# Forgetting attention: the requests' forget sums in a buffer of their own, split later, and the last quarter of output tile 0 moved

## The reference, cut to what matters

```
logf  = log_sigmoid(f_raw + f_bias)
f_cum = cumsum(concat([past_logf, logf], axis=1), axis=1)
s = einsum('bqhd,bkhd->bhqk', q, k) * scale
s = s + f_cum[query] - f_cum[key];  s = where(key <= query, s, -inf)
out = einsum('bhqk,bkhd->bqhd', softmax(s), v)
...
out = concat([c_out, d_out]) @ w_out
```

## Time and profile before

| | |
|---|---|
| median of three runs | 1737.83 us |
| lowest and highest run | 1737.72 and 1738.06 us |
| span of the profiled execution | 1735.7 us |
| mean granted TensorE clock in it | 1.000 |
| TensorE busy (matmul) | 98% of the span, 11360 instructions |
| VectorE, ScalarE, GpSimd busy | 61%, 39%, 21% |

### The profile page before, as it was taken

How to read it: one execution, slowest core, us unless ns; L and a number is a source line. 1 busy time by engine, 2 the same in 40 slices (tenths; PEclk the granted TensorE clock), 3 DMA queues, 4 the chain that set the end, 5 groups by cost and what they waited for, 6 DMA issues and landing times.

```text
span 1735.7 us, 27688 instructions
## 1 busy us (share of the span) xinstructions
PE 1702.0 (98%) x11360; PEld 1543.0 (89%) x11360; DVE 1058.7 (61%) x1717; ACT 683.9 (39%) x1219; POOL 370.5 (21%) x289
## 2 busy tenths in 40 slices
PE   7999998999999999999999999999999999999999
PEld 6566556797999999999989899789899999999999
DVE  3699867637667647465654424744676774655574
ACT  4111243435525525253552124633543453544352
POOL 3012100211104324132213132200110241414240
PEclk9999999999999999999999999999999999999999
DMA  8222330142303131403143221603320313122212
GB/s 263 101 77 103 93 107 28 49 195 98 104 27 138 32 130 46 135 19 128 31 141 74 75 73 64 246 27 114 153 93 25 128 48 115 61 70 86 87 66 91
DMA packets 39674, 162.30 MB, mean 94 GB/s; under 512 B 9384, under 2 KB 10280, under 8 KB 25600
## 3 DMA queue, kind: packets, MB, share of 16 engines
q1 hardware_dynamic: 32240, 124.59, 21.5%
q0 software_dynamic: 7312, 35.98, 5.8%
HBM read 149.87 MB, written 10.42 MB: 92 GB/s over the span
## 4 chain that ended last, share of the span: by engine, by line
PE 92%; DVE 5%; ACT 2%; issue 1%; DMA 0%; POOL 0%; SPq 0%; DVEq 0%; ACTq 0%
PE G L940 68%; PE S L940 11%; PE Q L940 11%; PE Q L1635 1%; ACT work L1731 0%; DVE rstd L2344 0%; DMA ring<-in_w_mk 0%; DVE ev_low L2593 0%; ACT rstd L1731 0%; DVE stats L2623 0%; DVE resid L2875 0%; ACT h_split L1731 0%; PE Q L1347 0%; DVE stats L2992 0%; DVE work L2636 0%
## 5 line engine op out<-in xcount | busy, mean ns | idle before, releaser
L940 PE MATMUL G<-ffn_rows,w_split 128*128 128x320 f32 x2160 | 329.8, 309 | 0.0
L940 PEld LDWEIGHTS G<-ffn_rows,w_split 128*128 128x128 f32 x2160 | 320.1, 188 | 0.0
L1731 ACT ACTIVATE w_split<-ring 128x512 fp32r<-128x512 f32 (+2 forms) x224 | 159.1, 711 | 316.8 <-PE G L940 208.4
L940 PE MATMUL G<-front,ring 128*128 128x128 f32 (+2 forms) x832 | 223.3, 430 | 11.0 <-DMA ring<-in_w_mk 9.3
L940 PEld LDWEIGHTS G<-front,ring 128*128 128x128 f32 x832 | 133.0, 193 | 100.0 <-issue 95.9
L856 POOL TENSOR_TENSOR mkT<-ring 128x512 f32<-128x512 f32 x72 | 98.2, 1369 | 564.6 <-DMA ring<-in_w_up 382.2
L940 PE MATMUL G<-h_split,w_split 128*128 128x320 f32 x1344 | 200.9, 310 | 1.2 <-DVE w_split L2359 0.8
L940 PEld LDWEIGHTS G<-h_split,w_split 128*128 128x128 f32 x1344 | 197.5, 188 | 1.9 <-issue 1.3
L940 PE MATMUL G<-g_split,w_split 128*128 128x320 f32 x1056 | 163.7, 310 | 0.1
L940 PEld LDWEIGHTS G<-g_split,w_split 128*128 128x128 f32 x1056 | 156.7, 188 | 1.7 <-DVE w_split L2848 1.4
L2715 DVE TENSOR_TENSOR w_split<-ring,w_split 128x512 fp32r<-128x512 f32 (+1 forms) x124 | 105.8, 854 | 59.9 <-ACT w_split L1731 58.7
(11 more groups left out here) (351 smaller groups left out, 2818.8 us busy)
## 6 DMA issues: line engine op xcount, KB each, us to landing
ring<-in_w_up SPq DMA_DIRECT2D x44, 1024.0 KB, 4.8
ring<-in_w_down SPq DMA_DIRECT2D x48, 256.0 KB, 2.6
ring<-in_w_down SPq DMA_DIRECT2D x32, 320.0 KB, 2.9
front<-in_mem_k POOLq DMA_DIRECT2D x8, 1024.0 KB, 6.1
front<-in_mem_v POOLq DMA_DIRECT2D x8, 1024.0 KB, 10.6
ring<-in_w_mk SPq DMA_DIRECT2D x4, 1024.0 KB, 5.9
ring<-in_w_mv SPq DMA_DIRECT2D x4, 1024.0 KB, 10.9
ring<-in_w_glu SPq DMA_DIRECT2D x4, 1024.0 KB, 8.6
```

Of the source, the lines that this page charges most:

```text
L940: return nc.tensor.matmul(out, lhsT, rhs, start=start, stop=stop, **kw)
L1731: return nc.scalar.activation(*a, **k)
```

## The change

The forget sums get a buffer `flog_rows` of their own. The cast to `run_forget` and the first `request_low` move from VectorE's work on tile 6 to round 2 of the attention loop, the second `request_low` and `request_queries` to round 3, and `query_blocks` to round 4; in each round they stand behind the maxima and the normalise and ahead of the results. Blocks 2 and 3 of output tile 0 move from round 21 to round 22 of TensorE's loop, behind the values of item 19. The descriptor scratch is set to 8192 bytes.

```diff
--- before.py
+++ after.py
@@ -288,6 +288,7 @@
         cdiag = sb("cdiag", [NH, NSEG, NH])
         decay = sb("decay", [P, NSEG, NH])
         toks = sb("toks", [P, 2, NCH, NH])
+        flog_rows = sb("flog_rows", [P, REQ // 2 * KPAIR])
         ARENA = 24064
         with nc.sbuf_tensor("front", [P, KD * T + ARENA], F32) as front:
 
@@ -483,7 +484,7 @@
         gate = [work[:, 2, :], work[:, 3, :]]
         p1, u2, u3, p5 = (work[:, i, b * (T // 2):(b + 1) * (T // 2)] for i in range(2) for b in range(2))
         wf = work[:, :, :].rearrange("p a b -> p (a b)")
-        flog = wf[:, 2 * T:2 * T + REQ // 2 * KPAIR].rearrange("p (r t) -> p r t", r=REQ // 2)
+        flog = flog_rows[:, :].rearrange("p (r t) -> p r t", r=REQ // 2)
         FLOG_ROWS = 64 + 32 + NH
         fP = [a.rearrange("p a b -> p (a b)").rearrange("p (e m) -> p e m", e=2) for a in (mv[:, 0], mkT[:, 0])]
         fPT = wf[:, 0:4 * 512].rearrange("p (b e m) -> p b e m", b=2, e=2)
@@ -1713,10 +1714,15 @@
                         fox_values(at)
                     else:
                         fox_run_turns(at)
-                if NFOX <= it < NFOX + 2:
+                if it == NFOX:
                     pe.wait_ge(od_rows, 4)
-                    pe.wait_ge(fox_exp, it - 1)
-                    odout_tile(NFOX + 1 - it, range(4))
+                    pe.wait_ge(fox_exp, NFOX - 1)
+                    odout_tile(1, range(4))
+                if it == NFOX + 1:
+                    pe.wait_ge(fox_exp, NFOX)
+                    odout_tile(0, range(2))
+                if it == NFOX + 2:
+                    odout_tile(0, range(2, 4))
             pe.wait_ge(value_read, len(VTILE))
             for i in range(8):
                 odout_tile(i, range(4 if i < 2 else 0, KD))
@@ -3062,16 +3068,11 @@
                 if j == 6:
                     fox_maxima(0)
                     fox_normalise(0)
-                    tile_wait(dve, TILE0["fqk"] + 7)
-                    own(v.tensor_copy(run_forget[0:FLOG_ROWS, :, :], flog[0:FLOG_ROWS, :, :]))
-                if j == 6:
-                    request_low(0)
                 if j < 7:
                     key_eps(j + 1)
                 if j == 6:
                     fox_maxima(1)
                 if j == 7:
-                    request_low(1)
                     fox_maxima(2)
                     fox_normalise(1)
                 norm([(fqk[:, FQK[j], :],) * 2], lambda _: small[:, 4:5] if FQK[j] < 4 else pr("fk"))
@@ -3127,8 +3128,13 @@
                 if 3 <= it <= NFOX:
                     fox_normalise(it - 1)
                 if it == 2:
+                    tile_wait(dve, TILE0["fqk"] + 7)
+                    own(v.tensor_copy(run_forget[0:FLOG_ROWS, :, :], flog[0:FLOG_ROWS, :, :]))
+                if it in (2, 3):
+                    request_low(it - 2)
+                if it == 3:
                     request_queries()
-                if it == 3:
+                if it == 4:
                     query_blocks()
                 for kind, at in VSTEPS[it]:
                     if kind == "values":
@@ -3286,7 +3292,7 @@
         "o_fk": (P, 4, T), "o_fv": (P, NCH, 512), "o_fl": (NH, T),
         "o_mk": (P, LAYERS, MH, MT), "o_mv": (P, LAYERS, 2, 512),
     }
-    nc = bacc.Bacc("TRN2", target_bir_lowering=False, num_devices=1)
+    nc = bacc.Bacc("TRN2", target_bir_lowering=False, num_devices=1, dynamic_dma_scratch_size=8192)
     arrays = {k: np.ascontiguousarray(v) for k, v in arrays.items()}
     arrays = {f"in_{k}": v for k, v in arrays.items()}
     dram = {k[3:]: nc.dram_tensor(k, v.shape, F32, kind="ExternalInput").ap() for k, v in arrays.items()}
```

## The result

| | before | after |
|---|---|---|
| median | 1737.72 us (5 runs, 1737.41 to 1738.06) | 1748.18 us (5 runs, 1747.41 to 1749.35) |
| span of the profiled execution | 1735.7 us | 1746.1 us |
| mean granted TensorE clock | 1.000 | 0.996 |

The changed kernel is slower by 10.5 us; the ratio is 1.0058, with an interval of 1.0047 to 1.0069. That is outside of the range given, on the side of rivals 3 and 4. Lines of the changed file are one higher for TensorE (L941 for L940) and mostly six higher for VectorE and ScalarE (L3132 and L3017 are now the cast and the low parts, L3034 `query_blocks`, L1737 ScalarE's helper).

The account below looks back on a forecast made before the run. TensorE, 92% of the chain, was taken to bound the kernel. + 2.35 at the head - 0.8 at the tail = + 1.55 us, from 1737.83 to 1739.4 us; range 1738.8 to 1740.1, with rivals 1 to 3 1736.5 to 1741.6.

Parts of the forecast that it names:

- rival 3: Behind the new 2.7 us pause at the attention's head TensorE's clock falls, costing 2.1 us: 1741.5 us; chance 0.08.
- rival 4: At the start GpSimd's small loads wait for descriptor room, 0.4 to 3.2 us come out, at worst 1742.6; chance 0.05.
- Part 2: Attention head: VectorE's moved work delays `query_blocks`, TensorE stands 2.7 us and starts item 5's scores 2.35 us later.
- Part 1: Attention head: without the cast and low parts ahead of `key_eps(7)`, the pipeline comes 0.33 us earlier.
- Part 3: Attention tail: moved matmuls fill TensorE's 0.72 us pause after item 19's values, winning 0.8 us.
- part 4: The rest: own buffer, moved tensors and other queues cost nothing, within 0.2 us; the halved scratch is left to a rival.
- The 1.93 us: At the start, the second memory key's idle wait for ScalarE on GpSimd, taken as the hidden part of rival 4's stop.
- Nothing gives the time back: Behind item 5's scores the 2.35 us delay stays, as TensorE runs almost without a pause to the tail.

Follow-up runs that it names:

- ring_only: The kernel before with only the descriptor scratch set to 8192 bytes: 1743.57 us against 1738.15, ratio 1.0032.
- head_784: The changed kernel with the tail as before and 12544 bytes of scratch, so the head's edit alone: 1744.42 us against 1738.14, ratio 1.0032.
- loads_later: The changed kernel (scratch 8192) with the eight xbc_state loads issued behind the four memory keys: 1743.59 us, ratio 1.0030.
- room_784: The changed kernel with 12544 bytes of descriptor scratch instead of 8192: 1744.10 us, ratio 1.0030.
- second_half_later: loads_later with the second low part and the part of `request_queries` for requests 4 to 7 moved to the end of round 7: 1742.57 us, ratio 1.0017.
- both_later: loads_later with `query_blocks` in round 3 and the second half of the request work at the end of round 7: 1736.80 us, ratio 0.9995.
- tail_only: The kernel before with only the tail's edit, blocks 2 and 3 of output tile 0 behind item 19's values: 1737.18 us against 1737.89, ratio 0.9994.
- blocks_round3: loads_later with `query_blocks` in round 3 instead of round 4, behind `request_queries`: 1738.24 us, ratio 0.9999.
- room_752: The changed kernel with 12032 bytes of descriptor scratch instead of 8192: 1750.67 us, ratio 1.0074.
- seven_first: ring_only with seven of the twelve small loads ahead of the memory keys and five behind them: 1737.90 us against 1738.14, ratio 1.0000.

## Why the prediction was wrong

**What held.** Part 2, the sum of VectorE's steps, came out to a tenth: the maxima of item 3, the second low part, `request_queries` and `query_blocks` follow one another at the intervals added up there, the pause was 2.77 us for 2.7, and the scores of item 5 came 2.5 us later for 2.35. Part 1 held too: `key_eps(7)` starts without the cast, the wait for it at the head is gone, found again as 0.65 us for ScalarE's logarithm, and the values of item 0 are 5.41 us later where the scores of item 1 were 5.73 us later, the 0.3 us of the forecast. Part 3 held: 0.7 us for 0.8, with the pause gone and nothing late. The sum on these three parts, + 1.55 us, was left with nothing for the two things that cost the rest. (The range is 0.3 us too wide at its upper end for its own bounds: 1737.83 + 2.7 - 0.72 = 1739.8, not 1740.1. It changes nothing here.)

**What failed, 1: part 4, "The halved descriptor scratch is priced as a rival", at 0.05 and with nothing in the sum.** The mechanism, the place and the load at which the queue would stop were written down as rival 4, with six loads instead of seven. Two of its steps failed. The first is the bound of the wait: the seventh "waits for the first to land", "at worst for the fourth", 2.4 to 5.1 us. The queue waited until the last load under way had landed, which was issued at 21.0 and took 10.0 us: 9.47 us of stop. The second is what is hidden. The 1.93 us were read on GpSimd's second key; but GpSimd's first key ended 9.0 us later (37.15 for 28.16) and TensorE's next group behind the pause started 4.55 us later (37.82 for 33.27), so about 4.4 us were hidden. The two errors go against each other: a stop of 9.47 less 1.93 would have been 7.5 us, and ring_only measured 5.4. That this pause too brings the low clock was not in rival 4, and most of that cost fell into the old wait of 1.82 us. For the chance of 0.05 the prediction names no row. By the earlier trace rows eight loads were issued before the first one landed at 22.7, and no row told how much room a load takes.

**What failed, 2: rival 3 at 0.08, with nothing in the sum.** "Nothing gives the time back" was right, but more was lost than the pause. The price was right in kind (2.1 us; 3.0 in the profiled execution, up to 4.6 elsewhere), the chance was not. The rival's own sentence, that the pause is longer than any in this stage, spoke for it, and the kernel before had no pause between 1.8 and 9 us that could have told. head_784 has a mean clock below 1 in all of its seven runs. The head cost 6.3 us, of which the predicted pause is 2.4.

Both rivals came true together, a case to which the prediction gave no time; its own prices would have made 1739.4 + 2.1 + 3.2 = 1744.7, still 3.5 us short.

**The sum.** 5.4 for the start and 5.4 for what loads_later keeps (pause, clock and tail) are 10.8; the changed kernel measured 10.5 above. That the two agree so well is in part luck: taken as the changed kernel less room_784 or less loads_later, the start is 4.1 or 4.6 us, as the low clock at the head differs by some us from run to run. The forecast held only the pause and the tail, 1.55.

**What stays open.** Where exactly the clock falls. Runs of one kernel differ (second_half_later 1738.1 to 1743.1), and in both_later the clock is a little low in 4 of 11 runs without any pause of over 1.1 us; in the kernel before this happened in 5 of 33 runs. With the old head and the new tail (tail_only) it happened in none of 11, with the new head and a short pause in 6 (blocks_round3) and in 4 (both_later). The new head has a longer wait for ScalarE ahead of the transposes of item 0 (0.65 us for 0.39), 1.1 us ahead of the wait of 1.11 us, which may be why; no run tests that. The 0.6 us between 122 and 1087 us weren't followed up either.

## What to carry to other kernels

A change that makes room in on-chip memory by shrinking the DMA scratch changes GpSimd's queue: add up the transfers that GpSimd issues, each at its number of pieces and also over idle stretches, and see which one fills the scratch and what is under way there, since a full queue here waited for the last of them. Put that place where nothing waits for GpSimd. Before work is moved behind a step, list what then stands in front of the first instruction that somebody waits for: the release of `run_ready` was the price, and the half that items 12 and 15 alone need could go four rounds later for nothing that can be told. A pause of TensorE in a stage without slack can cost more than its length: here the 2.4 us at the head cost 6.3, while the 4.8 us at the start, with an old wait behind it, cost 5.4.

## What the runs showed of the hardware

- Twelve loads of 1024 pieces each fit in 12544 bytes of scratch in each partition; with 12032 the twelfth waits for 11.33 us and with 8192 the eighth waits for 9.47 us (9.73 in ring_only). More room can be slower: with 12032 bytes the changed kernel lost 12.5 us to the kernel before, with 8192 bytes 10.5.
- In all four of these places that were looked at (after, ring_only, room_752, loads_later) the stopped load goes out 0.3 to 0.5 us behind the landing of the last load ahead of it. In loads_later the eighth load stops for 2.19 us though four of the seven had landed 8 us or more before, and in seven_first, where all seven had landed, it does not stop.
- Such a stop has no releaser in the profile. It stands under "issue" in front of a DMA issue of GpSimd; TensorE's wait behind it showed "issue" too, while ScalarE's named GpSimd.
- The clock fell to 0.50 in every profiled execution with a pause of TensorE of 4.8 to 6.5 us (after, ring_only, room_752) or of 2.5 to 2.8 us (five of them), during the longer pauses or at their end, and 0.5 to 1.6 us after the restart behind the shorter ones, and stayed low for some 3 to 10 us; with pauses of 1.5 us at most it fell in some runs and not in others of one kernel. Behind the 1.82 us pause at 42.6 us of the kernel before it did not fall.
